# Two-block network on one core: VectorE's order and the bank ring at the start of the seven-product chunks, one rounding moved forward in the mixing stages, and the modulation turned by transposes

## The chip, the core and the metric

The kernel runs on one core of a Trainium2 chip. The metric is the device time of one execution in microseconds (us). TensorE (PE) multiplies into PSUM, which has eight banks of 128 x 512 fp32 elements; VectorE (DVE), ScalarE (ACT) and GpSimd (POOL) do the elementwise work; SyncE (SP) issues the DMAs. Each engine runs its own instruction list in order and waits on semaphores.

## The reference

512 tokens of width 1024 in fp32 pass through two blocks. The first has a pooling and gating layer (also over 256 context tokens), then a Fourier and latent-attention layer. The second has two layers of feed-forward, mixing, feed-forward:

```
sh, sc, gt = split(silu(c) @ w_mod + b_mod, 3)          # modulation, for c and for c_ctx, once per first-block layer
h = x * (1 + sc) + sh
...
for l in range(2):                                        # second block
    f = (silu(n @ w_gate) * (n @ w_up)) @ w_down          # n = rmsnorm(x), 1024 -> 2816 -> 1024
    x = x + 0.5 * rmsnorm(f)
    x = x + rmsnorm(token_mixing(rmsnorm(x)))             # band, differential and stick-breaking attention
    x = x + 0.5 * rmsnorm(second feed-forward of rmsnorm(x))
```

## The kernel before

**Products in three parts.** Each fp32 operand of a large product is split into a rounded part (hi, cast to fp32r by ACT) and a remainder (lo, a DVE subtraction), and PE multiplies hi by hi, hi by lo and lo by hi. Weights come in chunks of 256 columns or rows (1 MB) through two `raw` tiles. A raw tile may be loaded again when DVE has made the lo part of the chunk in it. ACT's `split_at` makes hi (line 1548), DVE's `split_at` makes lo (line 2080).

**The feed-forward stage** (`ffn`, four times). `first_groups` computes the first gate chunk and the first up chunk in two halves of tokens. Chunk 1 of gate and of up is then done whole: four groups of 24 matmuls of 512 columns, in banks 0 to 3 (gate, gate, up, up). Chunks 2 to 10, gate and up in turn, are done with seven products of quarter blocks instead of eight: 18 chunks of 84 matmuls of 256 columns. Each such chunk opens three banks from a ring of eight, for products 1, 6 and 5, in the order 1, 6, 5, 7, 2, 3, 4. The ring's position is set just ahead (`rot.at = 2`, line 1323), so that the first of these chunks takes banks 2, 3 and 4. A bank is claimed when its last reader is done: gate groups are read by ACT (silu, line 1566), up groups by DVE (`up`, line 2577).

DVE's list at that start is: `up` of the first chunk's first half; in `first_groups`, lo of gate chunk 1, then `mix_tokens` (eight operations, lines 2591 to 2599: four sums that rebuild the fp32 tokens, then four that combine their quarter blocks), then `up` of the second half; lo of up chunk 1; lo of the combined tokens (line 2686, after ACT's rounding, line 1916); `first_mixed` (two sums of weight blocks, lines 2625 and 2627); lo of blocks A1 and A22 (line 2610); lo of the combinations S1, S2, S3, S4 (line 2618); and only then the two `up` operations of chunk 1. After that comes a loop over the 18 chunks in which DVE prepares the next chunk's weights and sums up the products of this one; ACT copies products out of PSUM (line 1900) and rounds.

**The mixing stage** (`mixing`, twice). Its order is written out by hand for each engine, a letter per step (`MIX_LETTERS`). Letters that matter here: p is a piece of a projection, b a turn of band probabilities (PE transposes) with ACT's copy of them, s and t the stick-breaking heads, a the band scores, k the copy of a projection out of its bank (ACT; projections use banks 0 and 1 in turn), w the splitting of the next weight chunk (ACT hi, DVE lo). ACT's list begins s a a w k k: score copies of a head pair, two exponentials, rounding of chunk 3, and the copies of the first two value projections.

**The modulation.** 24 pieces of 256 columns. `mod_product` leaves four partial sums, one in each group of 32 partitions; ACT copies them to `mod_row`. `mod_turn` (PE) multiplies each half of `mod_row` (128 x 128) by `mod_sum` (128 x 2, made by three DVE additions of columns of the identity), which sums the four groups and turns them in one: out come 2 columns for c and c_ctx. DVE adds the bias (line 2121). Eight pieces come ahead of the first projections, in four pairs; the other sixteen are spread over the projections of the first layer.

Of the kernel before, what the change touches and what calls it, by code (L numbers as in the profile page):

```python
# [11 lines left out]
ALU = mybir.AluOpType  # L12
AX = mybir.AxisListType

P = 128
# [159 lines left out]
def mix_streams():  # L175
# [27 lines left out]
    for letter, name, n in (("m", "assemble_norm", NT), ("l", "assemble_gain", NT), ("y", "out_end", NT), ("q", "square", NT - 1), ("r", "turn", NT - 1)):  # L203
# [14 lines left out]

MIX_LETTERS = {
    "pe": ("vppspspsaapbpbppppappbbppppcpcappppppppppcbcppcppttbppssbpdtpptppdfppadpssppsppcpppbpspspsfbpccpppabppppcppdpbafbdpppppc"  # L220
           "ssgttgttpffgdpcsspdpppcsdfspspsbbpppgappppfdggfdppdfpfdgpgpppfcdggppfdgcstbfdbggastfdccttssfabbsccabbgnfgccbbpcpaogcppnp"
           "pppppnbobppppppccooprpppnpppppppprppppr"),
    "act": ("saawkkatkkabbwkswkkaabbkbwkaakbkbddktfwsskkwkatsbadfksbkktwkkababdkdbgwfaktggffdksawkstsddtsbbfgkkfdgdgfwddggakfffaxgggf"
            "ddkwbfggxbfaaddtsbbfaastbbxngaafbgbwownyagaonbbqyoonqyrwqryr"),
    "dve": ("aataswaaawsccwtcacctwastsdtetddsswacewatssaatecccwdeadasscettttwdscsdcewdtseetaasddeeddewecddcseetdaatsdttcesscwaaeccaan"
            "xmxxlcccowwncmaalomymlnlcqcooynqrywqryr"),
    "pool": "stststmmymmqyqyqy",}


# [17 lines left out]
def build(nc, A, out):  # L247
# [3 lines left out]
    def sb(scope, name, shape, dt=F32):  # L251
        names[0] += 1
        return scope.enter_context(nc.sbuf_tensor(f"{name}_{names[0]}", shape, dt))

    with ctx:
        signals = []

        def signal(name, step=1):
            signals.append(Signal(ctx.enter_context(nc.semaphore(name)), step))
            return signals[-1]  # L260
# [28 lines left out]

        ln_put = signal("ln_put")  # L290
        swap_zeroed, slots_zeroed, q_turned = signal("rope_swap_zeroed"), signal("zero_rows_made"), signal("q_rope_put")
        mod_sum_made, silu_zeroed = signal("mod_sum_made"), signal("silu_zeroed")
        cols_made, mod_made, w_lo_made = signal("cols_made"), signal("mod_made"), signal("w_lo_made")
        scale_made, part_made, h_lo_made = signal("one_plus_scale_made"), signal("scaled_by_dve"), signal("h_lo_made")
        sgu_w_turned, diag_made, v_stats = signal("sgu_w_turned"), signal("gate_diag_made"), signal("v_stats_made")
# [19 lines left out]
        def bank(b, n=BANK, off=0):  # L315
            return psum[:, b * BANK + off:b * BANK + off + n]
# [48 lines left out]
        first = ExitStack()  # L365
        stats_first = sb(first, "stats_first", [P, 244])
        silu_c = sb(first, "silu_c", [P, KT, 32])
        mod_sum = sb(first, "mod_sum", [P, 2])
        mod_ab = sb(first, "mod", [P, 24, 2])
        mod_cd = sb(first, "mod_odd", [P, 24, 2])  # L370
        scale1 = sb(first, "one_plus_scale", [P, KT, 2])
# [416 lines left out]
        def tensor_program(pe):  # L788
# [53 lines left out]
            def mod_turn(n, b=None):  # L842

                event = ("modt", n)
                b = claim(rot.take() if b is None else b, event)
                if n == 0:
                    pe.wait_ge(*mod_sum_made["all"])
                pe.wait_ge(*mod_row_made[n])
                for j in range(2):
                    m = mm(bank(b, 2, 2 * j), mod_row[mod_turn_of(n) % 2][:, j * P:(j + 1) * P], mod_sum[:, :], True, True)  # L850
                done(m, event)

            def turn(kind, t, src, banks=None):
# [459 lines left out]
            def ffn(f, layer, before, more):  # L1313
# [3 lines left out]
                for c in range(1, FAST_FROM):  # L1317
                    for kind in ("gate", "up"):
# [1 line left out]
                        for j in range(2):  # L1320
                            project((kind, s, 2 * c + j, 0), w, j * P, P, h_hi, h_lo, 0, L, rot)
                        end((kind, f, layer, c))
                rot.at = 2
                for q, key in enumerate(fast_keys(f, layer)):
                    banks = {}
                    for product, name, to in FAST_ORDER:
# [747 lines left out]
        def vector_program(dve):  # L2074
# [27 lines left out]
                dve.tensor_scalar(a, a, scale / weight ** 2, EPS / weight ** 2, ALU.mult, ALU.add).then_inc(*biased.mark(event))  # L2102

            dve.memset(silu_c[:, :, :], 0.0).then_inc(*silu_zeroed.mark("all"))
            dve.wait_ge(*ident_landed["all"])
            dve.tensor_tensor(mod_sum[:, :], ident[:, 0:2], ident[:, 32:34], ALU.add).then_inc(*mod_sum_made.mark("first"))
            dve.wait_ge(*mod_sum_made["first"])
            dve.tensor_tensor(mod_sum[:, :], mod_sum[:, :], ident[:, 64:66], ALU.add).then_inc(*mod_sum_made.mark("second"))
            dve.wait_ge(*mod_sum_made["second"])
            dve.tensor_tensor(mod_sum[:, :], mod_sum[:, :], ident[:, 96:98], ALU.add).then_inc(*mod_sum_made.mark("all"))  # L2110
# [4 lines left out]
            def mod_turn(n):  # L2115
                dst, name, ch = mods(n)
                event = ("modt", n)
                if n == 0:
                    dve.wait_ge(*cols_made["all"])
                dve.wait_ge(*psum_full[event])  # L2120
                dve.tensor_tensor(dst[:, 2 * ch:2 * ch + 2, :], full(event, 4).rearrange("p (j s) -> p j s", s=2),
                                  col(name, 2 * ch, 2).unsqueeze(2).broadcast_to([P, 2, 2]), ALU.add).then_inc(*mod_made.mark(n))
                freed[event] = mod_made[n]

            def turn(kind, t, hi, lo, off, scale, shift):
                event = (kind, t, 1)
# [429 lines left out]
            def first_groups(before, sinks, split_after, then=None):  # L2556
                for half_ in range(2):
                    for n, sink in enumerate(sinks):
                        sink(half_)
                        if half_ == 0 and n == 1:  # L2560
                            turn_scale(before, 3)
                            turn_lo(before, 3)
                        if half_ == 1 and n == 1:
                            split_at(split_after)
                            if then:
                                then()

            def ffn(f, layer, before, more):
                s = ("ffn", f, layer)
# [12 lines left out]
                def mix_tokens():  # L2582

                    def block(k_half, half_):
                        return [t[:, 4 * k_half:4 * k_half + 4, half_ * quarter:(half_ + 1) * quarter].bitcast(F32) for t in (main_hi, main_lo)]

                    t1, t2, t3, t4 = [t_plain[:, i, :, :] for i in range(4)]
                    b11, b21 = [wide[i][:, :].rearrange("p (k n) -> p k n", k=4) for i in range(2)]
                    dve.wait_ge(*h_lo_made["rt", before, NT - 1, 1])
                    for dst, b in ((t1, block(0, 1)), (b11, block(0, 0)), (t3, block(1, 1)), (b21, block(1, 0))):  # L2590
                        m = dve.tensor_tensor(dst, b[0], b[1], ALU.add)
                    m.then_inc(*fast_t.mark(("plain", s)))
                    dve.wait_ge(*fast_t["plain", s])
                    dve.tensor_tensor(t3, t3, t1, ALU.subtract).then_inc(*fast_t.mark(("T3", s)))
                    dve.wait_ge(*fast_t["T3", s])
                    dve.tensor_tensor(t1, t1, b11, ALU.subtract)
                    dve.tensor_tensor(t2, t3, b11, ALU.add).then_inc(*fast_t.mark(("T2", s)))
                    dve.wait_ge(*fast_t["T2", s])
                    dve.tensor_tensor(t4, b21, t2, ALU.subtract).then_inc(*fast_t.mark(("mixed", s)))
# [88 lines left out]
                first_mixed(keys[0])  # L2688
                for name in ("A1", "A22"):
                    lo_blocks(keys[0], name)  # L2690
                for name in ("S1", "S2", "S3", "S4"):
                    lo_mixed(keys[0], name)
                for c in range(1, FAST_FROM):
                    for j in range(2):
                        up(2 * c + j, 0, 0, L)
                for q, key in enumerate(keys):
                    following = keys[q + 1] if q + 1 < len(keys) else None
                    if q:
# [363 lines left out]
```

## Time and profile before

| | before |
|---|---|
| median of 3 runs (lowest, highest) | 2636.1 us (2635.0, 2636.86) |
| the profiled execution's own time | 2636.2 us |
| its span in the profile | 2634.4 us |
| PE busy (share of the span) | 2577.5 us (98%) |
| DVE busy | 1685.8 us (64%) |
| ACT busy | 1166.5 us (44%) |
| POOL busy | 413.6 us (16%) |
| mean granted clock of TensorE | 0.996 |

The span is the time from the first to the last instruction in the profile. A row in the timeline gives start, length, engine, line, operation, output<-inputs and their form, and in brackets how long the engine had been idle and which engine's instruction ended that. Most matmuls are issued by helpers at line 804.

### The profile page before, as it was taken

To read this page: it belongs to the slowest core of one execution; us is meant where nothing else is said; L and a number is where in the kernel's file an instruction comes from. 1 tells how busy PE (TensorE), PEld (TensorE's weight loads), DVE (VectorE), ACT (ScalarE), POOL (GpSimd) and SP (SyncE) were. 2 spreads that over 40 slices of the span, in tenths; PEclk is the share of its full clock that TensorE was granted. 3 is DMA by queue.
4 is the path that set the end of the run, shared out by engine and by line. 5 is a ranking of instruction groups with operands and counts; after the bars stand their busy time and mean duration, and the time that the engine had idled before them with its cause. 6 is when DMAs were issued, how large, how long until landed. Compare 5 with 4: busy or idle time off the path is not lost.

```text
span 2634.4 us, 42217 instructions
## 1 busy us (share of the span) xinstructions
PE 2577.5 (98%) x17359; PEld 2233.8 (85%) x17359; DVE 1685.8 (64%) x2597; ACT 1166.5 (44%) x2013; POOL 413.6 (16%) x412
## 2 busy tenths in 40 slices
PE   7999999999999999999999999999999999999998
PEld 5888887678999888866899988899888876899987
DVE  3423653666999354467699935899444467699933
ACT  3222333552555334456455533455334456355522
POOL 0140000001233001110133200233000011133300
PEclk9999999999999999999999999999999999999999
DMA  9631241011333323112233322333233212133322
GB/s 301 212 133 48 65 129 41 24 53 52 111 108 102 107 84 113 49 49 81 80 97 98 112 97 95 99 110 111 98 96 101 65 49 81 57 97 97 114 101 74
DMA packets 213988, 249.59 MB, mean 95 GB/s; under 512 B 12879, under 2 KB 193702, under 8 KB 213798
## 3 DMA queue, kind: packets, MB, share of 16 engines
q1 hardware_dynamic: 213798, 246.90, 29.4%
q8 instruction: 139, 2.28, 0.4%
q14 instruction: 51, 0.42, 0.1%
HBM read 244.78 MB, written 2.10 MB: 94 GB/s over the span
## 4 chain that ended last, share of the span: by engine, by line
PE 90%; DVE 5%; ACT 2%; issue 2%; POOL 1%; DMA 0%; SPq 0%; DVEq 0%; POOLq 0%; ACTq 0%
PE psum L804 87%; PE psum L1374 1%; PE psum L1262 1%; PE psum L874 1%; DVE ff_hi L2686 1%; DMA mod_w<-in_ab_w_mod 0%; ACT w_hi L1548 0%; DVE stats_first L2167 0%; DVE work L2160 0%; DVE w_lo L2610 0%; DVE w_lo L2080 0%; POOL stats_first L2881 0%; DVE X L2163 0%; ACT work L1589 0%; DVE ff_hi L2618 0%
## 5 line engine op out<-in xcount | busy, mean ns | idle before, releaser
L804 PE MATMUL psum<-h_hi,w_hi 128*128 128x256 f32 (+1 forms) x1520 | 499.8, 329 | 10.0 <-DVE ff_plain L2577 8.1
L804 PE MATMUL psum<-h_lo,w_hi 128*128 128x256 f32 (+1 forms) x1520 | 492.1, 324 | 0.0
L804 PE MATMUL psum<-h_hi,w_lo 128*128 128x256 f32 (+1 forms) x1520 | 492.0, 324 | 0.0
L2080 DVE TENSOR_TENSOR w_lo<-raw,w_hi 128x2048 fp32r<-128x2048 f32 (+1 forms) x102 | 230.4, 2263 | 320.8 <-ACT w_hi L1548 320.7
L804 PEld LDWEIGHTS psum<-h_hi,w_hi 128*128 128x128 f32 x1520 | 291.1, 192 | 44.8 <-DVE ff_plain L2577 9.8
L804 PEld LDWEIGHTS psum<-h_hi,w_lo 128*128 128x128 f32 x1520 | 291.3, 192 | 22.7
L804 PEld LDWEIGHTS psum<-h_lo,w_hi 128*128 128x128 f32 x1520 | 291.4, 192 | 19.7 <-issue 0.5
L1548 ACT ACTIVATE w_hi<-raw 128x2048 fp32r<-128x2048 f32 (+1 forms) x102 | 192.4, 1889 | 258.1 <-PE psum L804 247.4
L804 PE MATMUL psum<-w_hi,ff_hi 128*128 128x512 f32 x576 | 224.9, 390 | 1.2 <-DVE ff_lo L2678 1.2
L804 PE MATMUL psum<-w_lo,ff_hi 128*128 128x512 f32 x576 | 224.1, 389 | 0.0
L804 PE MATMUL psum<-w_hi,ff_lo 128*128 128x512 f32 x576 | 224.1, 389 | 0.0
L804 PE MATMUL psum<-ff_hi,w_hi 128*128 128x256 f32 x1152 | 213.2, 283 | 0.0
L2610 DVE TENSOR_TENSOR w_lo<-raw,w_hi 128x1024 fp32r<-128x1024 f32 (+1 forms) x144 | 210.5, 1503 | 0.0
L1888 ACT ACTIVATE w_hi<-raw 128x1024 fp32r<-128x1024 f32 (+1 forms) x144 | 120.9, 842 | 180.0 <-PE psum L804 180.0
L804 PEld LDWEIGHTS psum<-ff_hi,w_hi 128*128 128x128 f32 x1152 | 179.3, 191 | 0.0
L804 PE MATMUL psum<-w_hi,h_hi 128*128 128x256 f32 (+2 forms) x512 | 166.5, 325 | 4.7 <-ACT v_a L1566 3.4
L1900 ACT ACTIVATE wide<-psum 128x256 f32<-128x256 f32 x288 | 110.4, 383 | 129.0 <-PE psum L804 127.8
L804 PE MATMUL psum<-ff_hi 128*128 128x256 f32 (+1 forms) x992 | 167.4, 300 | 0.0
L804 PE MATMUL psum<-ff_hi,w_lo 128*128 128x256 f32 x576 | 162.9, 283 | 0.0
L804 PE MATMUL psum<-w_lo,h_hi 128*128 128x256 f32 (+2 forms) x512 | 159.5, 312 | 0.0
L804 PE MATMUL psum<-w_hi,h_lo 128*128 128x256 f32 (+2 forms) x512 | 159.4, 311 | 0.0
L804 PEld LDWEIGHTS psum<-ff_hi 128*128 128x128 f32 x992 | 135.4, 195 | 5.0
(366 smaller groups left out, 5466.2 us busy)
## 6 DMA issues: line engine op xcount, KB each, us to landing
raw<-in_ffn_w_gate SPq DMA_DIRECT2D x44, 1024.0 KB, 5.4
raw<-in_ffn_w_up SPq DMA_DIRECT2D x44, 1024.0 KB, 5.4
raw<-in_ffn_w_down SPq DMA_DIRECT2D x44, 1024.0 KB, 4.9
raw<-in_w_in SPq DMA_DIRECT2D x36, 512.0 KB, 5.0
raw<-in_ab_w_in SPq DMA_DIRECT2D x10, 1024.0 KB, 7.8
mod_w<-in_ab_w_mod SPq DMA_DIRECT2D x8, 1024.0 KB, 12.0
raw<-in_w_out SPq DMA_DIRECT2D x8, 1024.0 KB, 5.0
raw<-in_cd_w_in SPq DMA_DIRECT2D x7, 1024.0 KB, 6.1
```

Source lines behind the costliest of these rows:

```text
L804: return pe.matmul(o, lhsT, rhs, start=start, stop=stop, skip_group_check=True)
L874: m = pe.transpose(bank(b, P, j * P), wide[1][:, k * P:(k + 1) * P], ident[:, :])
L1262: m = pe.transpose(bank(b + k // 4, P, (k % 4) * P), probs[(n - 1) % 2][:, k * P:(k + 1) * P], ident[:, :])
L1374: m = pe.transpose(bank(b, P, k * P), src[:, k * P:(k + 1) * P], ident[:, :])
L1548: act.activation(split_tiles(key)[0][:, 0:nk * n], raw[c % 2][:, 0:nk * n], ACT.Copy).then_inc(*w_hi_made.mark(key))
L1888: act.activation(dst, src, ACT.Copy).then_inc(*w_hi_made.mark((key, name)))
L1900: act.activation(fast_stage(q, name), bank(b, quarter), ACT.Copy).then_inc(*fast_kept.mark((s, q, name)))
L2080: dve.tensor_tensor(lo[:, 0:nk * n], raw[c % 2][:, 0:nk * n], hi[:, 0:nk * n].bitcast(F32), ALU.subtract).then_inc(*w_lo_made.mark(key))
L2610: dve.tensor_tensor(dst, src, hi.bitcast(F32), ALU.subtract).then_inc(*w_lo_made.mark((key, name)))
L2686: m = dve.tensor_tensor(t_lo[:, i, :, :], t_plain[:, i, :, :], t_hi[:, i, :, :].bitcast(F32), ALU.subtract)
```

## The change

Six edits:

1. `mod_turn` on PE: two transposes of 128 x 128 against the identity in place of the two matmuls; `mod_sum` and its three additions go. On DVE each turn now takes two small reductions (each over the four partition groups, now four groups of columns, of 2 output elements), a wait on them, and the bias addition in place.
2. `rot.at` is 0 instead of 2 ahead of the seven-product chunks.
3. In a feed-forward stage, DVE's lo of gate chunk 1 moves from ahead of `mix_tokens` to behind its sixth operation.
4. DVE's two `up` operations of chunk 1: the first goes between S2 and S3, the second stays behind S4.
5. In the mixing stages the rounding of chunk 3 (w) moves to the front of ACT's list, ahead of s a a, and in DVE's list from sixth to third place.
6. In PE's mixing list one projection piece (p) goes ahead of a pair of turns (b b) instead of behind it.

```diff
 MIX_LETTERS  pe:   (middle of the second string)
-  ...pcsdfspspsbbpppgappppfdgg...
+  ...pcsdfspspspbbppgappppfdgg...
 MIX_LETTERS  act:
-  "saawkkatkkabb...
+  "wsaakkatkkabb...
 MIX_LETTERS  dve:
-  "aataswaaawscc...
+  "aawtasaaawscc...
@@ mod_turn, TensorE
-                if n == 0:
-                    pe.wait_ge(*mod_sum_made["all"])
                 pe.wait_ge(*mod_row_made[n])
                 for j in range(2):
-                    m = mm(bank(b, 2, 2 * j), mod_row[...][:, j * P:(j + 1) * P], mod_sum[:, :], True, True)
+                    m = pe.transpose(bank(b, P, P * j), mod_row[...][:, j * P:(j + 1) * P], ident[:, :])
@@ ffn, TensorE
-                rot.at = 2
+                rot.at = 0
@@ mod_turn, VectorE
-                dve.tensor_tensor(dst[:, 2 * ch:2 * ch + 2, :], full(event, 4)..., col(...).broadcast_to([P, 2, 2]), ALU.add)
-                freed[event] = mod_made[n]
+                for j in range(2):
+                    m = dve.tensor_reduce(dst[:, 2 * ch + j, :], full(event, P, P * j).rearrange("p (g c) -> p c g", g=4)[:, 0:2, :], AX.X, ALU.add)
+                m.then_inc(*mod_made.mark(("sum", n)))
+                freed[event] = mod_made["sum", n]
+                dve.wait_ge(*mod_made["sum", n])
+                dve.tensor_tensor(out_, out_, col(name, 2 * ch, 2).unsqueeze(2).broadcast_to([P, 2, 2]), ALU.add)
@@ first_groups, VectorE
                         if half_ == 1 and n == 1:
-                            split_at(split_after)
                             if then:
                                 then()
+                            else:
+                                split_at(split_after)
@@ mix_tokens, VectorE
                     dve.tensor_tensor(t1, t1, b11, ALU.subtract)
+                    split_at(CHUNK["gate", f, layer, 1])
                     dve.tensor_tensor(t2, t3, b11, ALU.add)
@@ ffn, VectorE
-                for name in ("S1", "S2", "S3", "S4"):
+                for name in ("S1", "S2"):
                     lo_mixed(keys[0], name)
-                for c in range(1, FAST_FROM):
-                    for j in range(2):
-                        up(2 * c + j, 0, 0, L)
+                up(2 * FAST_FROM - 2, 0, 0, L)
+                for name in ("S3", "S4"):
+                    lo_mixed(keys[0], name)
+                up(2 * FAST_FROM - 1, 0, 0, L)
```

## Rows read from the trace of the kernel before

**Rows 1.** The page's first part: busy us, share of the span, instructions.

```profile
PE 2577.5 (98%) x17359; PEld 2233.8 (85%) x17359; DVE 1685.8 (64%) x2597; ACT 1166.5 (44%) x2013; POOL 413.6 (16%) x412
```

**Rows 2.** TensorE's waits: for whom, us in total, times, longest.

```profile
PE psum L804 <- DVE ff_plain L2577: 8.1, 4, 2.0
...
PE psum L804 <- ACT v_a L1566: 3.4, 2, 1.7
```

**Rows 3.** Timeline of TensorE at the second feed-forward stage's chunk starts.

```profile
1312.79 0.50 PE L804 MATMUL psum<-h_hi,w_hi 128*128 128x512 f32 x1 [0.32 <-DVE w_lo L2080]
...
1326.00 0.38 PE L804 MATMUL psum<-h_hi,w_hi 128*128 128x256 f32 x1 [2.02 <-DVE ff_plain L2577]
```

**Rows 4.** TensorE by stretches: us, busy, granted clock, DMA share, GB/s.

```profile
1328.00:1330.00 2.00, 2.00 (x11) 0.50 1.03 362
...
1682.20:1684.20 2.00, 2.00 (x19) 1.00 1.05 370
```

**Rows 5.** Chain that ended last, seven-product stretches of stages two and three.

```profile
1326.00 181.53 PE psum L804 x1500
...
1680.18 180.03 PE psum L804 x1500
```

**Rows 6.** Timeline of VectorE at the second feed-forward stage.

```profile
1298.12 2.29 DVE L2080 TENSOR_TENSOR w_lo<-raw,w_hi 128x2048 fp32r<-128x2048 f32 x1 [7.55 <-ACT w_hi L1548]
1300.33 1.22 DVE L2591 TENSOR_TENSOR ff_room<-h_hi,h_lo 128x1024 f32<-128x1024 f32 x1
...
1307.39 1.22 DVE L2597 TENSOR_TENSOR ff_room<-ff_room,wide 128x1024 f32<-128x1024 f32 x1
...
1314.14 4.63 DVE L2686 TENSOR_TENSOR ff_hi<-ff_room,ff_hi 128x1024 fp32r<-128x1024 f32 x4 [1.42 <-ACT ff_hi L1916]
...
1323.46 1.88 DVE L2618 TENSOR_TENSOR ff_hi<-ff_room,ff_hi 128x512 fp32r<-128x512 f32 x3
1325.27 1.27 DVE L2577 TENSOR_TENSOR ff_plain<-work,psum 128x512 f32<-128x512 f32 x2
...
1332.52 0.76 DVE L2633 TENSOR_TENSOR wide<-wide 128x256 f32<-128x256 f32 x2 [0.85 <-ACT wide L1900]
```

**Rows 7.** VectorE's waits in the window 1346 to 1500 us.

```profile
DVE wide L2665 <- PE psum L804: 2.7, 8, 0.3
```

**Rows 8.** Timeline of ScalarE at the first mixing stage's start.

```profile
1013.59 1.08 ACT L1566 ACTIVATE log_weights<-psum 128x512 f32<-128x512 f32 x2 [2.10 <-PE psum L804]
...
1020.39 1.90 ACT L1548 ACTIVATE w_hi<-raw 128x2048 fp32r<-128x2048 f32 x1
```

**Rows 9.** Timeline of VectorE at the same place.

```profile
1019.87 1.48 DVE L2815 SCALAR_TENSOR_TENSOR softplus<-log_weights 128x1280 f32<-128x1280 f32 x1
...
1023.46 2.28 DVE L2080 TENSOR_TENSOR w_lo<-raw,w_hi 128x2048 fp32r<-128x2048 f32 x1
```

**Rows 10.** Timeline of TensorE in the same mixing stage, the pair of turns.

```profile
1162.61 0.85 PE L1374 MATMUL psum<-ident,wide 128*128 128x128 f32 x6 [0.56 <-ACT log_weights L1566]
```

**Rows 11.** Timeline of TensorE: a modulation turn; two transposes between projections.

```profile
112.62 0.61 PE L804 MATMUL psum<-mod_sum,mod_row 128*128 128x2 f32 x4
113.09 0.36 PE L804 MATMUL psum<-ctx_hi,w_hi 128*128 128x256 f32 x1
...
392.16 0.29 PE L1142 MATMUL psum<-ident,work 128*128 128x128 f32 x1
...
392.31 0.32 PE L804 MATMUL psum<-w_hi,h_hi 128*128 128x160 f32 x1
```

**Rows 12.** Timeline of TensorE ahead of the first projections.

```profile
39.76 1.02 PE L804 MATMUL psum<-mod_sum,mod_row 128*128 128x2 f32 x8 [1.00 <-ACT mod_row L1566]
40.64 1.07 PE L932 MATMUL psum<-ident,X 128*128 128x128 f32 x8
```

**Rows 13.** The bias addition (instructions that use this tile), and VectorE's wait beside it.

```profile
L2121 DVE TENSOR_TENSOR mod<-psum,cols x12: 151/161/163, 20.8 to 95.0; 128x4 f32<-128x4 f32 x12
...
91.08 0.89 DVE L2273 BATCH_NORM_STATS2 stats_first<-psum 128x6 f32<-128x128 f32 x4 [0.43 <-PE psum L804]
```

More of the change, by code:

```diff
@@ L220 @@
     "pe": ("vppspspsaapbpbppppappbbppppcpcappppppppppcbcppcppttbppssbpdtpptppdfppadpssppsppcpppbpspspsfbpccpppabppppcppdpbafbdpppppc"
-           "ssgttgttpffgdpcsspdpppcsdfspspsbbpppgappppfdggfdppdfpfdgpgpppfcdggppfdgcstbfdbggastfdccttssfabbsccabbgnfgccbbpcpaogcppnp"
+           "ssgttgttpffgdpcsspdpppcsdfspspspbbppgappppfdggfdppdfpfdgpgpppfcdggppfdgcstbfdbggastfdccttssfabbsccabbgnfgccbbpcpaogcppnp"
            "pppppnbobppppppccooprpppnpppppppprppppr"),
[L223 to L226, printed above, removed]
+    "act": ("wsaakkatkkabbwkswkkaabbkbwkaakbkbddktfwsskkwkatsbadfksbkktwkkababdkdbgwfaktggffdksawkstsddtsbbfgkkfdgdgfwddggakfffaxgggf"
+           "ddkwbfggxbfaaddtsbbfaastbbxngaafbgbwownyagaonbbqyoonqyrwqryr"),
+    "dve": ("aawtasaaawsccwtcacctwastsdtetddsswacewatssaatecccwdeadasscettttwdscsdcewdtseetaasddeeddewecddcseetdaatsdttcesscwaaeccaan"
+           "xmxxlcccowwncmaalomymlnlcqcooynqrywqryr"),
     "pool": "stststmmymmqyqyqy",}
@@ L291, in build @@
         swap_zeroed, slots_zeroed, q_turned = signal("rope_swap_zeroed"), signal("zero_rows_made"), signal("q_rope_put")
-        mod_sum_made, silu_zeroed = signal("mod_sum_made"), signal("silu_zeroed")
+        silu_zeroed = signal("silu_zeroed")
         cols_made, mod_made, w_lo_made = signal("cols_made"), signal("mod_made"), signal("w_lo_made")
@@ L367, in build @@
         silu_c = sb(first, "silu_c", [P, KT, 32])
-        mod_sum = sb(first, "mod_sum", [P, 2])
         mod_ab = sb(first, "mod", [P, 24, 2])
@@ L845, in mod_turn @@
                 b = claim(rot.take() if b is None else b, event)
-                if n == 0:
-                    pe.wait_ge(*mod_sum_made["all"])
                 pe.wait_ge(*mod_row_made[n])
                 for j in range(2):
-                    m = mm(bank(b, 2, 2 * j), mod_row[mod_turn_of(n) % 2][:, j * P:(j + 1) * P], mod_sum[:, :], True, True)
+                    m = pe.transpose(bank(b, P, P * j), mod_row[mod_turn_of(n) % 2][:, j * P:(j + 1) * P], ident[:, :])
                 done(m, event)
@@ L2104, in vector_program @@
             dve.memset(silu_c[:, :, :], 0.0).then_inc(*silu_zeroed.mark("all"))
[L2105 to L2110, printed above, removed]
             dve.wait_ge(*psum_full["vecs"])
@@ L2120, in mod_turn @@
                 dve.wait_ge(*psum_full[event])
-                dve.tensor_tensor(dst[:, 2 * ch:2 * ch + 2, :], full(event, 4).rearrange("p (j s) -> p j s", s=2),
-                                  col(name, 2 * ch, 2).unsqueeze(2).broadcast_to([P, 2, 2]), ALU.add).then_inc(*mod_made.mark(n))
-                freed[event] = mod_made[n]
+                out_ = dst[:, 2 * ch:2 * ch + 2, :]
+                for j in range(2):
[3 more added lines that the diff above has]
+                dve.wait_ge(*mod_made["sum", n])
+                dve.tensor_tensor(out_, out_, col(name, 2 * ch, 2).unsqueeze(2).broadcast_to([P, 2, 2]), ALU.add).then_inc(*mod_made.mark(n))
             def turn(kind, t, hi, lo, off, scale, shift):
```

## The prediction

> **What bounds the kernel now.** I read the page's first part, then TensorE's waits, then the timelines of TensorE, VectorE and ScalarE around each place that the diff touches. TensorE is busy for 2577.5 of 2634.4 us [rows 1]: it is the bound, and only two things can shorten the run: idle time of TensorE that goes, and TensorE work that goes. VectorE's or ScalarE's work matters only where TensorE waits for it. The waits show two of the places concerned: 8.1 us in four waits of 2.0 for `up` (line 2577), and 3.4 us in two waits for the copies of the value projections [rows 2]. The timeline of TensorE adds a wait of 0.32 us for lo of up chunk 1, which stands at each of the four feed-forward stages, and one of 0.56 us in front of a pair of turns, once in each mixing stage [rows 3, 10].
>
> The stall of 2.0 us costs more than itself. Behind it, in the second feed-forward stage, the granted clock is 0.50, the lower level of 1.2 GHz, where it was 2.4 GHz ahead of it; at the same distance behind the third stage's stall it is 1.00 [rows 4]. The 18 chunks take 181.53 us in the one and 180.03 in the other [rows 5]: the lower clock costs 1.5 us. The first and the fourth stage look like the second. On this the Trainium skill ("TensorE: Matmul & The Clock Gate", "What's actually happening") says that the activity window runs freely and is not tied to the kernel, so that the same program can see its clock change at different points; that three equal stalls of four lose the clock agrees. By that rule other stalls may gain or lose such a dip in the new kernel by mere position; no step below counts on it.
>
> **Edits 2 and 4: the first seven-product chunk (four times).** TensorE ends chunk 1 at 1326.00 - 2.02 = 1323.98 and needs bank 2, which holds the first `up` group; VectorE reads that at 1325.27, the last but one of its list [rows 3, 6]. With the ring at 0 product 1 opens bank 0, a gate group that ScalarE copied long before, product 6 bank 1, the other gate group, and product 5 bank 2. A chunk is 180.03 / 18 = 10.0 us, a product 1.43 [rows 5]. So bank 2 is needed at 1323.98 + 2.9 = 1326.9, and VectorE, whose list in front of S3 is what it was (lo of the tokens starts at 1314.14, held by ScalarE's rounding, which is not moved), reads it between S2 and S3: S1 and S2 end at about 1324.1 [rows 6] (S2, S3 and S4, the three of line 2618, take 1.88 us), `up` takes 0.64, free at 1324.8. What is late next: product 6 needs S2 at 1323.98 + 1.43 = 1325.4, 1.3 us after it is there. The second `up`, S3 and S4 end within 0.7 us of where they did, and their readers come later. So the stall goes whole: 4 x 2.0 = 8.1 us, and with it three dips of 1.5: 4.5 us. Bounds: nothing, if the next condition comes as late; 8.1 + 4 x 1.5 = 14.1 above.
>
> Does VectorE keep up with a TensorE that is 3.5 us earlier? It waits 2.7 us in 154 us of this stretch, always for TensorE [rows 7], so it is nearly full. In the first chunk it has waits of 0.85 [rows 6], 0.65 and 0.69 us for ScalarE and TensorE, which vanish: VectorE moves forward by 2.2 of the 3.5. Its lead shrinks by 1.3 us. I estimate that lead, from when S2 of a chunk is made to when product 6 reads it, at 3 us in the tightest chunks by the two timelines, so 1.7 are left. I count nothing. The weight DMAs on SP's queue wait for S4's lo, 0.6 us later once, against 10 us per chunk. The GpSimd sums of the second chunk wait for the second `up`, whose place does not move. At the far end the ring gives the down product banks 3 to 5 from the last chunk instead of 5 to 7; they are claimed some 4 us after the stage's start, and VectorE frees them within 1.
>
> **Edit 3 (four times).** VectorE waits 7.55 us for ScalarE's hi of gate chunk 1, then does lo and the eight operations [rows 6]. Six of these, 1307.39 - 1300.33 = 7.1 us, fit into that wait with 0.4 to spare, so lo of gate chunk 1, which TensorE needs a microsecond after it is made, stays where it is. Behind it only two are left, so lo of up chunk 1 comes some 6 us earlier, bounded by ScalarE's rounding of it, and the wait of 0.32 us goes: 1.3 us in all. If the six took 0.4 us more than the wait they would still be hidden by the microsecond; the price beyond is one for one, four times. SP may load the next raw tile those 6 us earlier, at a quiet time.
>
> **Edit 5 (twice).** ScalarE is idle for 2.10 us ahead of the score copies at 1013.59; its rounding of chunk 3 takes 1.90 [rows 8]. Tile and slot are free by then (the slot's last reader is the group that ends at 1011.1), so it fits with 0.2 us to spare. The copy of the first value projection then starts at 1020.39 instead of behind the rounding, and the wait of 1.7 us goes. On VectorE lo of chunk 3 (2.28 us) now stands in front of the absolute value of head 1 at 1019.87 and of the next band scores [rows 9]; behind these ScalarE waits, and behind it the copy of the third value projection, which I find at 1027.8, when TensorE asks for it at 1027.75. So a wait of 0.1 may come back: gain 1.6 each, 3.3 in all. Bounds: 0 (the head's chain is later by the full 2.28 and is waited for) and 3.4. In between ScalarE and VectorE wait for TensorE many times in this stage, so what TensorE gains is carried to its end.
>
> **Edit 6 (twice).** The turns wait 0.56 us for a bank that ScalarE is still copying [rows 10]. A projection piece of six matmuls of 512 columns ahead of them covers it. The turns come 0.8 us later, and ScalarE's copy of them with it, needed two steps on. 1.1 us; bounds -0.6 and 1.1.
>
> **Edit 1 (24 turns).** A turn is four passes, since each fp32 matmul takes two, and 113.09 - 112.62 = 0.47 us to the next matmul; two transposes between projections take 392.31 - 392.16 = 0.15 [rows 11]. In the sixteen turns among the projections, where TensorE is never idle, this is 16 x 0.32 = 5.1 us. The first eight come in pairs: the pair at 39.76 takes 0.88 us [rows 12], two pairs of transposes about 0.3; but the second turn of a pair then waits for ScalarE's copy, and the pair's end is followed by VectorE's longer chain. I take 0.9 for all four pairs, between 0 and 2.3. Sum 6.0. The Trainium skill ("TensorE: Matmul & The Clock Gate", "Terms") has fp32 transposes four times faster in transpose mode; by that a turn would fall from 0.47 to 0.12, and 16 of them save 5.6 instead of 5.1.
>
> VectorE gets two reductions of 8 elements, with no row of their own; nearest is the addition of 4 elements, 0.16 us [rows 13]. At 0.16 to 0.3 each with the wait, a turn adds 0.35 to 0.65 us. Queued behind it in the value steps are the statistics of the value groups, ahead of which VectorE idles 0.43 us [rows 13] in a step of 4.5 us. TensorE's step shrinks by 0.3, so VectorE may fall behind by 0.2 to 0.5 per step for six steps, against 1.4 us until a bank is missed. Cost 0 to 1.5; I take 0.
>
> **Sum.** 8.1 + 4.5 + 1.3 + 3.3 + 1.1 + 6.0 = 24.3 us. The profiled execution took 2636.2 us, 1.8 more than its span and 0.1 more than the median. 2636.2 - 24.3 = 2611.9, and 2611.8 on the median's side.
>
> **Rivals.**
> A. Only part of the stall at the seven-product chunks goes: the next condition (S2, or the bank of product 5) comes late because VectorE's small operations stretch, or the clock drops there anyway. For it: VectorE is full there. Against: 1.3 and 2.1 us of margin. Half of 12.6 lost: 2618.
> B. The modulation or the mixing edit gives nothing: VectorE's longer turn becomes the value steps' bound, or head 1's later chain is waited for. For it: 0.43 us of room in the one, 0.05 in the other. 4 to 6 us lost: 2617.
> C. Slower: in the seven-product stretches VectorE, 98% full [rows 7], can't hold a TensorE that leaves it 1.3 us less lead, and each chunk ends late. It decides from 24.3 / 68 = 0.36 us per following chunk; at 0.5 the time is 2611.9 + 34 = 2646. Against it: VectorE's work per chunk is unchanged, and a lead once lost costs once, not per chunk.
> D. The change does not do what it says: the bank stays late since another holder stands in it, and the other edits are hidden; no change, 2636.
> E. More than forecast: other dips of the clock, 1.5 us each by [rows 5], go by position as well, and the first eight turns give their upper bound: 2607.
>
> **How the numbers follow.** Forecast 62%, A 15%, B 10%, C 4%, D 3%, E 6%. The forecast's own range, from the small bounds of edits 1 and 5, is 2608 to 2616; A, B, E and the far bounds of the single edits take it to 2603 and 2623, which leaves out C and D. A measurement of this kernel tells 0.2% (5 us) from no change. Faster by more: forecast, A, B, E: 93%; within: 3%; slower: 4%.
>
> **What would show it.** In TensorE's waits the entry for line 2577 gone, and no clock under 1.00 behind the four starts; the 18 chunks at 180.0 us in all four stages; no 0.32 wait at up chunk 1; the 3.4 us for the value copies down to under 0.4; modulation turns of two transposes at 0.15 to 0.2 us. The forecast is wrong if VectorE's waits for TensorE in the seven-product stretches vanish for good and TensorE waits there instead, if the saving of edit 1 is under 3 us at 243 us into the span, or if a wait on VectorE's lo of the next weights appears in the mixing stages.

## The result and the profile after

The changed kernel took 2614.2 us, the median of four runs (2613.2 to 2615.3), against 2636.0 (2635.0 to 2636.9) for the kernel before on the same chip. The ratio is 0.9918, 95% interval 0.990 to 0.9935: 21.8 us faster. The profiled execution took 2613.2 us with a span of 2611.4, which is 23.0 less than the span of before. That is the likeliest case of the prediction, 2.4 us short of its sum.

Lines of the changed kernel are numbered a little lower: line 804 of before is 803, line 2577 is 2573. The page's first part of the changed kernel, answering to [rows 1]:

```profile
PE 2566.0 (98%) x17311; PEld 2222.6 (85%) x17311; DVE 1690.3 (65%) x2642; ACT 1168.0 (45%) x2013; POOL 420.8 (16%) x412
```

TensorE's waits in the changed kernel, cut to what is new (for whom, us in total, times, longest). The waits of [rows 2] are in the list no more:

```profile
PE psum L847 <- ACT mod_row L1563: 1.8, 3, 1.2
...
PE psum L803 <- DVE work L2138: 1.6, 1, 1.6
```

The second feed-forward stage again, where [rows 3] had its waits of 0.32 and 2.02 us. The timeline of TensorE passes from the last group of 512 columns to product 1 without a stop:

```profile
1313.98 0.39 PE L803 MATMUL psum<-h_hi,w_lo 128*128 128x512 f32 x1
1314.20 0.28 PE L803 MATMUL psum<-h_hi,w_hi 128*128 128x256 f32 x1
```

VectorE's timeline at the same place, answering to [rows 6]: S1, S2, the first `up`, S3 and S4, the second `up`:

```profile
1305.16 4.63 DVE L2683 TENSOR_TENSOR ff_hi<-ff_room,ff_hi 128x1024 fp32r<-128x1024 f32 x4 [8.24 <-ACT ff_hi L1913]
...
1313.88 0.68 DVE L2615 TENSOR_TENSOR w_lo<-w_plain,w_hi 128x512 fp32r<-128x512 f32 x1
1314.48 0.68 DVE L2615 TENSOR_TENSOR ff_hi<-ff_room,ff_hi 128x512 fp32r<-128x512 f32 x1
1315.08 0.67 DVE L2573 TENSOR_TENSOR ff_plain<-work,psum 128x512 f32<-128x512 f32 x1
1315.68 1.28 DVE L2615 TENSOR_TENSOR ff_hi<-ff_room,ff_hi 128x512 fp32r<-128x512 f32 x2
1316.89 0.67 DVE L2573 TENSOR_TENSOR ff_plain<-work,psum 128x512 f32<-128x512 f32 x1
```

The granted clock behind the start (us, busy of the engines, clock, DMA share, GB/s) is the upper level, 2.4 GHz, where [rows 4] had 0.50; and VectorE's waits for TensorE in 1320 to 1486 us, against 2.7 in [rows 7], show that it still keeps up:

```profile
1316.00:1318.00 2.00, 2.00 (x19) 2.00 (x18) 2.00 (x4) 1.13 (x3) 0.27 (x1) 1.00 0.00 0
```

```profile
DVE wide L2662 <- PE psum L803: 1.7, 5, 0.3
```

**Where the 23.0 us came from.** Four kinds of instruction mark the same point in every variant of the kernel: TensorE's first projection matmul, its first pooling product of 256 columns (behind a wait of 2.14 us), the first turn of a stage, and the first matmul of a down product. In the timeline of TensorE of the changed kernel two of them read so:

```profile
1267.30 0.95 PE L871 MATMUL psum<-ident,wide 128*128 128x128 f32 x7 [0.24 <-DVE wide L2188]
...
1495.87 0.47 PE L803 MATMUL psum<-w_hi,ff_hi 128*128 128x512 f32 x1 [0.31 <-DVE ff_lo L2675]
```

The kernel before has them at 1276.30 and 1509.25, so the stretch took 232.95 us before and 228.57 after: 4.38 gained. Likewise for the rest, all from the timelines of TensorE:

| stretch | gained, us | forecast |
|---|---|---|
| first projection to pooling (modulation) | 3.0 | 6.0 |
| start of feed-forward stages 1, 2, 3, 4 | 4.37, 4.38, 2.91, 4.42 = 16.1 | 13.9 |
| mixing stages 1, 2 | 2.18, 2.32 = 4.5 | 4.4 |
| elsewhere (start-up, pooling) | -0.6 | 0 |

From a stretch that an edit does not touch, two kernels differ by 0.05 us, 0.16 at worst (the first stretch, in which the clock moves, and what follows it are excepted), so the stretches measure an edit far better than the medians do. I use them below as "the stretch".

### The profile page after: what moved, and what is told of

It reads as the page before. It is cut to its first block, busy times and chain, and to the rows that moved or that the text cites. A ratio compares the mean times of both kernels' runs of the same rounds, so it can differ in the third digit from the quotient of the medians.

```text
span 2611.4 us, 42166 instructions
## 1 busy us (share of the span) xinstructions
PE 2566.0 (98%) x17311; PEld 2222.6 (85%) x17311; DVE 1690.3 (65%) x2642; ACT 1168.0 (45%) x2013; POOL 420.8 (16%) x412
## 4 chain that ended last, share of the span: by engine, by line
PE 92%; DVE 3%; ACT 2%; issue 1%; POOL 1%; DMA 0%; SPq 0%; POOLq 0%; DVEq 0%; ACTq 0%
PE psum L803 89%; PE psum L1371 1%; PE psum L1259 1%; PE psum L871 1%; DMA raw<-in_ab_w_in 0%; ACT w_hi L1545 0%; DVE stats_first L2162 0%; DVE work L2155 0%; DVE w_lo L2077 0%; POOL stats_first L2879 0%; DVE X L2158 0%; ACT work L1586 0%; PE psum L847 0%; DVE wide L2188 0%; POOL stats L2934 0%
```

## The experiments

All are the changed kernel with one edit, but for e9. Four starts means the starts of the seven-product chunks.

**e1: the ring at bank 2 again.**

```diff
-                rot.at = 0
+                rot.at = 2
```

> The changed kernel with the ring at bank 2 again where the seven-product chunks begin; the order of the two `up` operations stays the new one. In the trace of the changed kernel TensorE is ready for product 1 at 1314.20 us, VectorE's first `up` runs at 1315.08 to 1315.75 and the second at 1316.89 to 1317.5. So both theories expect a wait of about 1.5 us for bank 2 at each of the four starts and about 0.3 us for bank 3 one product later, 1.8 together and 2.1 with the overlap of two matmuls (0.17) that each stop takes. Theory 1 (a stall of this size costs its own length only): 2614.2 + 4 x 2.1 = 2622.6 us, clock 1.00 behind all four starts. Theory 2 (such a stall loses the clock as the stall of 2.0 did, 1.5 us each, in three of four places): 2627 us, windows with a clock under 1.00 some 2 to 4 us behind the starts. Rival (the ring does not matter once `up` is earlier): 2614.

Measured 2622.0 us (2620.9 to 2624.0), ratio to before 0.9947 (0.9932 to 0.9962). The timeline of TensorE:

```profile
1318.60 0.39 PE L803 MATMUL psum<-h_hi,w_hi 128*128 128x256 f32 x1 [1.45 <-DVE ff_plain L2573]
```

The four stretches are longer by 2.06, 2.09, 2.11 and 2.09 us, and no window behind a start has a clock under 1.00. Of the 2.1 us, 1.6 is the stop with the overlap; product 6 begins 1.80 us behind product 1 instead of 1.44, when the second `up` ends. Theory 1 stands: the ring position is worth 2.1 us per start, and a stop of 1.45 us lost no clock.

**e2: both `up` behind S4 again, the ring at 0.**

```diff
-                for name in ("S1", "S2"):
-                    lo_mixed(keys[0], name)
-                up(2 * FAST_FROM - 2, 0, 0, L)
-                for name in ("S3", "S4"):
+                for name in ("S1", "S2", "S3", "S4"):
                     lo_mixed(keys[0], name)
-                up(2 * FAST_FROM - 1, 0, 0, L)
+                for c in range(1, FAST_FROM):
+                    for j in range(2):
+                        up(2 * c + j, 0, 0, L)
```

> The changed kernel with the ring at 0 but both `up` operations behind S4 again. Theory (the ring alone removes the stall): bank 2 is opened by product 5, 2 x 1.44 = 2.9 us behind product 1, at 1317.1 us in the second stage; S1 to S4 end at about 1316.3 and `up` at 1316.95, so it is free with 0.1 us to spare and the time is that of the changed kernel, 2614.2 us, within 0.5. Rival (both halves are needed): a wait for bank 2 at product 5, 0.1 to 0.7 us at each of the four starts, 2615 to 2617, without a fall of the clock; if a wait that small also lost the clock, 2620.

Measured 2614.4 us (2614.1 to 2615.1), and the four stretches differ from the changed kernel's by 0.02 to 0.05 us. Edit 4 is worth nothing beside edit 2: the ring alone gives `up` enough time.

**e3: the modulation turned by matmuls again** (edit 1 undone whole, `mod_sum` back).

```diff
-                    m = pe.transpose(bank(b, P, P * j), mod_row[...][:, j * P:(j + 1) * P], ident[:, :])
+                    m = mm(bank(b, 2, 2 * j), mod_row[...][:, j * P:(j + 1) * P], mod_sum[:, :], True, True)
```

> The changed kernel with the turns of the modulation rows as matmuls against the summing columns again, and the old single addition on VectorE. Theory (the traces of the two kernels compared): the sixteen turns among the projections take 0.47 us instead of 0.20, 4.3 us together, the first eight 0.5 us more, and the wait of 1.56 us at the first gate row is gone; so the pooling stage is reached 2.8 us later than in the changed kernel and the time is 2617.0 us. Rival (what the modulation gained was position, not the turns): 2614 to 2615. The prediction's own figure would be 2620.2.

Measured 2616.1 us (2615.5 to 2616.7), 1.8 more than the changed kernel. The 1.56 us wait is gone. The stretch from the first projection to the pooling is 4.13 us longer, more than expected, and the next one, to the first turn, 1.78 shorter; only part of that is the turns. From the modulation product behind the first projections (33.79 us in the changed kernel) to the first gate row, where no clock falls, e3 takes 141.29 us like the kernel before, and the changed kernel 138.30: edit 1 is worth 3.0 there. Another 1.2 us lies ahead of that product, and most of the 1.78 is a fall of the clock. TensorE's windows at the pooling products, of the changed kernel and of e3:

```profile
244.00:248.00 4.00, 3.44 (x9) 2.47 (x9) 4.00 (x10) 2.12 (x5) 0.00 (x0) 0.60 0.77 262
```

```profile
248.00:252.00 4.00, 3.44 (x15) 2.55 (x16) 4.00 (x9) 2.13 (x5) 0.00 (x0) 1.00 0.70 262
```

The same waits (2.14 and 0.56 us) lost the clock in the one and not in the other. Without that fall the stretch behind the pooling is shorter by 1.45 us in e7 and 1.47 in e12, so some 0.3 of e3's 1.78 is left for the old turns; the kernel before, which has the fall, is 0.29 us shorter there too. Edit 1 thus loses 0.3 us again behind the pooling; what costs it was not looked into. And the 36 matmuls of the first projections took 7.2 us in the changed kernel and 8.4 in e3, though nothing in them differs; the last section says why.

**e4: GpSimd still while VectorE makes the low part and the gate diagonals.**

```diff
+                if g == 2:
+                    pool.wait_ge(*psum_full["gate", 0, 0])
                 for r, (off, n) in enumerate(RANGES):
                     o, a = PAD_OFF[r] - window // 2, ...
```

> The changed kernel with one more wait on GpSimd: in its third pooling group the division by the counts waits until TensorE has done the first gate row, so that GpSimd is still while VectorE makes the low part of the weights and the gate diagonals (167 to 172 us). Theory (GpSimd and VectorE slow each other where they overlap): that low part takes 2.3 us instead of 3.11, the eight diagonals 1.65 instead of 2.59, TensorE's wait of 1.56 us at the first gate row is gone, GpSimd's operations behind it take 1.09 and 0.64 us; 2612.6 us. Rival 1 (the diagonals are late because their place in VectorE's order is too near to TensorE's need): the durations come back but a wait of over 1 us stays, 2614. Rival 2 (the delayed counts hold back the weight loads queued behind them): the wait is gone and another, for a DMA, takes its place, 2614 or more.

The new wait of 1.6 us stands in front of the first gate row. First the changed kernel: VectorE, then GpSimd, then TensorE.

```profile
162.28 1.49 DVE L2118 TENSOR_TENSOR mod_odd<-mod_odd,cols 128x4 f32<-128x4 f32 x1
...
165.37 0.16 DVE L2118 TENSOR_TENSOR mod_odd<-mod_odd,cols 128x4 f32<-128x4 f32 x1
167.11 3.11 DVE L2077 TENSOR_TENSOR w_lo<-raw,w_hi 128x2048 fp32r<-128x2048 f32 x1 [1.58 <-ACT w_hi L1545]
170.14 2.59 DVE L2138 TENSOR_SCALAR work<-ident,mod 128x128 f32<-128x128 f32 x8
```

```profile
162.25 3.08 POOL L2897 TENSOR_TENSOR window_sums<-window_sums 128x789 f32<-128x789 f32 x2
...
166.78 1.29 POOL L2904 TENSOR_TENSOR pool_in<-window_sums,pool_in 128x512 f32<-128x512 f32 x1
168.03 2.78 POOL L2902 TENSOR_TENSOR window_sums<-window_sums,inv_count 128x256 f32<-128x256 f32 x1
170.89 0.78 POOL L2904 TENSOR_TENSOR pool_in<-window_sums,pool_in 128x256 f32<-128x256 f32 x1
```

```profile
172.09 1.10 PE L803 MATMUL psum<-work,ones 128*128 128x512 f32 x2 [1.56 <-DVE work L2138]
```

With the pause (VectorE, then TensorE):

```profile
168.85 2.29 DVE L2077 TENSOR_TENSOR w_lo<-raw,w_hi 128x2048 fp32r<-128x2048 f32 x1 [1.57 <-ACT w_hi L1545]
171.06 1.65 DVE L2138 TENSOR_SCALAR work<-ident,mod 128x128 f32<-128x128 f32 x8
```

```profile
172.12 1.06 PE L803 MATMUL psum<-work,ones 128*128 128x512 f32 x2
...
194.24 1.19 PE L803 MATMUL psum<-work,ones 128*128 128x512 f32 x1 [3.53 <-DVE work L2138]
```

The theory holds where it was put to the test: 3.11 falls to 2.29 us, 2.59 to 1.65, and the wait is gone. As a remedy it fails: GpSimd's fourth group now runs beside the third set of diagonals, and TensorE waits 3.53 us there; behind that stop the granted clock is 0.50 in the window from 193.4 to 200.1 us. Measured 2617.9 us (2614.4 to 2619.6). Rival 2 named a DMA for the new wait. Its first half came true, since the counts' DMA releases GpSimd's fourth group at 182.05 us instead of 175.69, but TensorE waits for VectorE's diagonals: it was the same contention, later. The first rows show how the two engines share: VectorE's addition of 4 elements, 0.16 us otherwise, ends with GpSimd's sum that began 0.03 us ahead of it (1.50 us, the first of the two in its row), and GpSimd's 256 columns, 0.74 us otherwise, which begin behind VectorE's low part, end 0.6 us after it (170.81 and 170.22). On this the Trainium skill ("SBUF — State Buffer", "SBUF: two separate sides") says that VectorE with two SBUF inputs and GpSimd take a common port pair as an exclusive lock for the whole instruction, first come, first served (and likewise VectorE's 2-port modes); these rows agree.

**e5: the first gate diagonals ahead of the low part on VectorE.**

```diff
                 elif kind == "split":
+                    if step[1] == 5:
+                        dve.wait_ge(*mod_made[11])
+                        gate_diags(("gate", 0, 0), mod_ab, 0, 0)
                     split_at(CHUNK["ab_in", step[1]])
...
-                    if s == h == 0:
-                        dve.wait_ge(*mod_made[11])
-                    gate_diags(step, mod_ab, h, s)
+                    if s or h:
+                        gate_diags(step, mod_ab, h, s)
```

> The changed kernel with the first gate diagonals on VectorE ahead of the low part of the weights at 167.11 us instead of behind it. Theory (only the diagonals' lateness costs; they may be stretched beside GpSimd but are then made by 168.2 us, against a need at 170.5): the wait of 1.56 us at the first gate row is gone, with the 0.17 us by which two matmuls overlap 1.7 us, so the pooling stage is reached 1.7 us earlier and the time is 2612.5 us. Rival 1 (the loss moves on: a TensorE that is 1.7 us earlier meets the later diagonals beside GpSimd's next sums): a wait for line 2138's diagonals at about 190 us, 2614. Rival 2 (the low part, later by 1.6 to 2.6 us, is now waited for at chunk 5): 2614 to 2615.

Measured 2613.3 us (2612.8 to 2614.1); the stretch to the pooling is only 0.45 us shorter. Rival 1: the wait at 172 us is gone and another is at 191.54, in front of the third set, which VectorE makes beside GpSimd. VectorE's and TensorE's timelines:

```profile
187.17 2.48 DVE L2077 TENSOR_TENSOR w_lo<-raw,w_hi 128x2048 fp32r<-128x2048 f32 x1 [13.29 <-ACT w_hi L1545]
189.58 2.60 DVE L2138 TENSOR_SCALAR work<-ident,mod 128x128 f32<-128x128 f32 x8
```

```profile
191.54 1.10 PE L803 MATMUL psum<-work,ones 128*128 128x512 f32 x2 [1.17 <-DVE work L2138]
```

**e6: the low part of gate chunk 1 ahead of the eight operations** (edit 3 undone: `split_at` back ahead of `then()` and out of `mix_tokens`).

> The changed kernel with VectorE's low part of gate chunk 1 ahead of the eight operations on the token blocks again. Theory (a stop of TensorE costs its length and the 0.17 us by which two matmuls overlap): the wait of 0.32 us for the low part of up chunk 1 is back in all four feed-forward stages, 0.5 each, 2616.2 us. By the prediction's own price, 0.32 each, it would be 2615.5. Rival (the wait came from the old order elsewhere and stays away): 2614.2.

Measured 2617.0 us (2616.5 to 2617.7). The waits are back, four of 0.32 among these five, and the four stretches are longer by 0.58, 0.62, 0.67 and 0.62 us:

```profile
PE psum L803 <- DVE w_lo L2077: 1.6, 5, 0.3
```

A wait of 0.32 costs 0.62 us, nearly twice its length. Part of that is how the timeline counts: an idle time begins at the modelled end of the last matmul, and in an unbroken run the ends overlap the next start by 0.17 us (0.39 us of one against 0.22 to the next, above). The rest is about the slow first matmul behind a stop, 0.50 us in [rows 3] against 0.39 for the others of 512 columns.

**e7: the mixing stages' rounding at its old places** (edit 5 undone).

```diff
-    "act": ("wsaakkatkkabb...
+    "act": ("saawkkatkkabb...
-    "dve": ("aawtasaaawscc...
+    "dve": ("aataswaaawscc...
```

> The changed kernel with the rounding of weight chunk 3 of the mixing stages at its old places in ScalarE's and VectorE's lists; TensorE's new order stays. Theory: the wait of 1.7 us for the copy of the first value projection is back in both mixing stages, with the overlap 1.85 each, 2617.9 us. Rival 1 (TensorE's new order alone had moved the wait elsewhere): 2614 to 2616. Rival 2 (without the early rounding the projection piece that was moved ahead of the turns has to wait too): over 2618.5.

Measured 2616.9 us (2616.4 to 2618.7). The wait is back, and the two stretches are longer by 1.75 and 1.77 us, 0.1 each less than expected:

```profile
PE psum L803 <- ACT v_a L1563: 3.4, 2, 1.7
```

**e8: the projection piece behind the turns** (edit 6 undone: `spspspbbpp` back to `spspsbbppp`, as in the diff of the change).

> The changed kernel with the projection piece of the mixing stages behind the pair of turns again. Theory: the wait of 0.56 us ahead of the turns is back in both stages, with the overlap 0.7 each, 2615.7 us. Rival (the earlier rounding has moved ScalarE so that the bank is free in time): 2614.2.

Measured 2615.3 us (2614.1 to 2617.1). The waits are back at 0.56 us each; the two stretches are longer by 0.49 and 0.53, not by 0.7. So the surcharge that e6 showed does not hold in the mixing stages; what gives it back there was not looked into:

```profile
PE psum L1371 <- ACT log_weights L1563: 1.1, 2, 0.6
```

**e9: the kernel before with the ring at bank 0 alone.**

```diff
-                rot.at = 2
+                rot.at = 0
```

> The kernel of before with the ring at bank 0 where the seven-product chunks begin, and nothing else. Theory (the ring alone removes the stall, 2.3 us each, and with it the fall of the clock, 1.5 us in three of four stages; the other edits are separate): TensorE's wait for line 2577 is gone, no clock under 1.00 behind the four starts, 2636.3 - 4 x 2.3 - 3 x 1.5 = 2622.6 us. Rival 1 (in the old order, with the tokens' low part some 1 us later against TensorE, a wait of 0.1 to 0.7 for S2 or bank 2 is left): 2623 to 2626. Rival 2 (the falls of the clock had another cause): 2627 us with windows under 1.00 at the old places.

Measured 2623.7 us (2621.9 to 2624.1), ratio 0.995 (0.9934 to 0.9967). The four stretches are 0.59 to 0.62 us longer than the changed kernel's, which is edit 3; against before they are shorter by 3.8, 3.8, 2.3 and 3.8. No wait for line 2577 and no clock under 1.00 behind the starts. One digit gives 13.7 us in these four stretches; by the medians, 13.3.

**e10: the old stall in the changed kernel** (e1 and e2 together) **and e11: the ring at bank 3**, so that product 1 waits for the second `up`.

> The changed kernel with both the ring at bank 2 and the two `up` operations behind S4 again, so that the old stall of about 2 us is back, 9 to 20 us earlier in the run than in the kernel before. Theory 1 (a stall of 2.0 is long enough to lose the clock, one of 1.45 is not): waits of 2.0 to 2.6 at the four starts and falls of the clock behind most of them, 2.3 to 2.8 us each and 1.5 for two to four falls, 2614.2 + 10 + 4.5 = 2628.7 us (2626 to 2631). Theory 2 (the falls behind the stalls went by position in the run alone, and the other edits moved them): the stalls without falls, 2624 us.

> The changed kernel with the ring at bank 3 where the seven-product chunks begin: product 1 then needs the bank of the second `up` group, which VectorE frees at 1317.5 us against a need at 1314.2. All theories expect one wait of about 3.2 us at each of the four starts, 3.4 with the overlap. Theory 1 (a longer stall loses the clock at every start): 2614.2 + 4 x (3.4 + 1.5) = 2633.8 us. Theory 2 (the clock falls at a place in the run and not behind a stall): 2614.2 + 13.6 = 2627.8 us.

Measured 2630.4 us (2628.5 to 2632.6) and 2632.9 (2630.0 to 2637.5). TensorE's windows behind the first, second, third and fourth start of e10:

```profile
680.00:684.00 4.00, 4.00 (x31) 4.00 (x31) 4.00 (x3) 1.29 (x3) 2.94 (x2) 0.84 0.67 232
1322.00:1326.00 4.00, 4.00 (x36) 4.00 (x35) 4.00 (x3) 1.94 (x5) 3.24 (x2) 1.00 0.68 238
...
1676.00:1680.00 4.00, 4.00 (x28) 4.00 (x28) 3.13 (x4) 1.27 (x4) 2.19 (x1) 0.75 0.39 134
2316.00:2320.00 4.00, 4.00 (x21) 4.00 (x22) 3.96 (x5) 0.90 (x2) 2.73 (x2) 0.57 0.82 261
```

The four stops of e10, 2.65 us each, lengthened the stretches by 4.16, 2.91, 4.44 and 4.41: the second start kept the clock, where before it was the third. In e11, with stops of 3.25, it was 4.80, 3.49, 5.02 and 3.51: two of four kept it. Neither of the two theories is right as put. A stop is needed (none of the starts without one, and none of the four with 1.45 us, has a fall; nor has any of the six waits of 1.7 us for the value copies in the kernel before, e7 and e9), but stops of 2.0 to 3.3 us lost the clock in 8 of 12 places, and which place is spared changes with the position in the run. That is the rule of a free-running window that the prediction cited from the Trainium skill ("TensorE: Matmul & The Clock Gate", "What's actually happening"), and these runs agree with it. A fall costs 1.3 to 1.5 us (4.16 - 2.91 and 5.02 - 3.50).

**e12: the first and the third set of diagonals ahead of their low parts.**

```diff
                 elif kind == "split":
+                    if step[1] == 5:
+                        dve.wait_ge(*mod_made[11])
+                    if step[1] in (5, 8):
+                        gate_diags(("gate", step[1] // 8, 0), mod_ab, 0, step[1] // 8)
                     split_at(CHUNK["ab_in", step[1]])
...
-                    if s == h == 0:
-                        dve.wait_ge(*mod_made[11])
-                    gate_diags(step, mod_ab, h, s)
+                    if h:
+                        gate_diags(step, mod_ab, h, s)
```

> The changed kernel with two sets of gate diagonals, the first and the third, on VectorE ahead of the low parts of the weights that stood in front of them; both are then made in idle time of VectorE. Theory (the wait that moved from 172 to 191 us when only the first set was moved is the third set, late behind a low part): both waits are gone, the pooling stage is 1.7 us nearer to the first projection than in the changed kernel, 2612.5 us. Rival (the loss moves on again, to the fourth set or to a low part): a wait of 0.5 to 1.5 us between 180 and 205 us, 2613 to 2614. That the start of the kernel differs by a microsecond from run to run may cover either.

Measured 2612.5 us (2609.4 to 2612.8), ratio to before 0.9905 (0.989 to 0.992). TensorE goes through the first and the third gate row without a wait:

```profile
170.08 1.02 PE L803 MATMUL psum<-work,ones 128*128 128x512 f32 x2
...
188.48 1.02 PE L803 MATMUL psum<-work,ones 128*128 128x512 f32 x2
```

From the product at 33.5 us to the first gate row it takes 136.58 us, against 138.30 in the changed kernel and 141.29 before. The span is 2607.6; of the 3.8 us under the changed kernel's, 1.5 is a clock that did not fall at the pooling products. The medians (2612.5 against 2614.2, with intervals of the ratio that overlap) would not have told the two apart; the stretch does. It is the fastest version here.

## Why the prediction was right in sum, and where its steps were wrong

The sum was met in part by luck. By the stretches, the starts of the feed-forward stages gave 2.2 us more than forecast, edit 1 gave 3.0 less and 0.6 were lost elsewhere; the mixing stages met theirs. These errors nearly cancel, and 24.3 us forecast stand against 23.0 by the spans.

**Edits 2 and 4 (12.6 forecast).** Right in mechanism: bank 2 was the whole condition, the next one is not late, the dips went with the stall, and VectorE kept up. The size was too small: the stall of 2.02 us and what is lost around it is 2.3 per start (the third, which had no fall, gained 2.91, of which 0.6 is edit 3), so 9.2 + 3 x 1.5 = 13.7 where 12.6 stood. And the credit was put wrong: edit 4 contributes nothing (e2), edit 2 alone 13.7 (e9). The prediction's own rows could have shown it: the old order freed bank 2 at 1325.27 + 0.64 = 1325.9 us, and with the ring at 0 it is needed at 1326.9.

**Edit 3 (1.3 forecast).** Right place, half the size: 4 x 0.62 = 2.5 (e6). Together with the term above the prediction took the length of an idle time for its price; the four starts gave 16.1 instead of 13.9.

**Edits 5 and 6 (3.3 and 1.1).** 3.5 (e7) and 1.0 (e8). The wait of 0.1 that the prediction thought possible at the third value projection did not come.

**Edit 1 (6.0 forecast): the step that failed.** The prediction said that it would be wrong "if the saving of edit 1 is under 3 us at 243 us into the span". The first pooling product of 256 columns comes 2.84 us earlier (246.55 and 243.71), 3.0 from the first projection on, of which 0.3 is lost again behind the pooling (e3). Three of its terms were off. The turn itself, two transposes in TensorE's timeline of the changed kernel:

```profile
110.25 0.44 PE L847 MATMUL psum<-ident,mod_row 128*128 128x128 f32 x2
110.44 0.37 PE L803 MATMUL psum<-ctx_hi,w_hi 128*128 128x256 f32 x1
```

It takes 0.19 us to the next matmul, against 0.47 in [rows 11]: 16 x 0.28 = 4.5 and not 5.1. The prediction's estimate by the factor of four in the Trainium skill ("TensorE: Matmul & The Clock Gate", "Terms") was 0.12; the section does not say against what the factor holds, and the measurement decides. The first eight turns were to give 0.9: the pair at 20 us gave nothing, since TensorE then waits 2.4 us for ScalarE instead of 1.9, and the later ones some 0.2, since their three waits for ScalarE's copy grew from 1.2 us (1.00 in [rows 12] and two of 0.12) to 1.8. And "Cost 0 to 1.5; I take 0" for VectorE was wrong at a place it did not name: not in the value steps, but at the first gate row. TensorE was through with the last turn ahead of it 4.6 us earlier (169.45 and 164.82), and with it VectorE's low part (171.64 and 167.11); GpSimd's third group, released by the DMA of its counts, came only 2.2 us earlier (162.88 and 160.66). So the low part slid under GpSimd's sums. That cost 1.56 + 0.17 = 1.7 us. Without it the modulation gives 4.7 from the product at 33.8 us on (e12), which is 4.5 and 0.2.

**The rivals.** A, C and D did not occur. B's first half did in part, by another mechanism: 3 us, of which 1.7 is that wait. E: the falls of the clock at the pooling and at 640 us stayed, 3.5 us earlier, and gave nothing.

## What to carry to other kernels

In an unbroken run of TensorE an idle time cost 0.3 us more than the timeline gives it (in the mixing stages it did not), and a fall of the clock behind it may add 1.5: a stop of 2 us cost 3.8. Ask first which bank a new phase opens: claiming one that has long been free was worth 13 of 22 us and one digit. When an edit moves one engine and not another, look for the pair VectorE and GpSimd that it brings together, and place what TensorE waits for ahead of long operations, in time where VectorE is idle.

## What the runs showed of the hardware

Beside a running GpSimd operation VectorE's 4-element addition took 1.49 us instead of 0.16, its 2048-column subtraction 3.11 instead of 2.29, and four diagonals 2.95 (e5) instead of 0.87 (e12). In the other direction GpSimd's 256-column product took 2.78 instead of 0.74.

The granted clock fell behind stops of 2.0 to 3.3 us in 8 of 12 places and behind stops of 1.45 in none of 4, and the same code at the same stop (2.14 and 0.56 us at the pooling products) fell in the changed kernel and not in e3; of the fourteen profiles, four (e3, e7, e9, e12) kept it there. The ten runs of e11 spread over 7.5 us, as much as five such falls, where the changed kernel's four spread over 2.1.

Behind the first projection's wait of 0.9 us, matmuls of 256 columns stood 0.21 us apart before they came down to 0.12, for 3.4 us in the kernel before and 5.7 in e3, while the windows there show a granted clock of 1.00. It was the clock all the same. In these profiles the clock's records begin only where the distance comes down (29.9 us in the kernel before, 32.6 in e3), and ahead of them the column shows 1.00. Only e2's records begin earlier, at 21.4 us. Its matmuls of 256 columns stand the same 0.21 us apart, the clock there is 0.50, and both change at 31.6 us. The windows of e2 and of the kernel before:

```profile
26.00:30.00 4.00, 3.24 (x15) 3.24 (x16) 3.00 (x3) 0.83 (x1) 0.00 (x0) 0.50 1.10 348
```

```profile
26.00:34.00 8.00, 7.62 (x44) 6.76 (x48) 2.62 (x2) 0.39 (x1) 0.00 (x0) 1.00 1.09 348
```

When the clock comes up differs from run to run, from 2.9 us behind the first projection (e10) to 6.0 (e7), and with it the same 36 matmuls take 7.1 to 8.5 us: time matmuls by their distance, not by the clock column alone.
